# A one-core decoder step: one expert's overflow moved into the last expert step, expert positions swapped by a table, slot table built only when needed

## Chip, cores, metric

One NeuronCore of a Trainium2 chip runs the whole step as one program. The metric is the device time of one execution in microseconds (us), as a median over runs. All numbers of the trace come from one profiled execution.

## The reference, cut to what matters

One hybrid decoder layer over 576 tokens (512 prompt, 64 sample) with 1024 channels, all in float32. A token mixer comes first. Then comes the part that the change touches, a mixture of 16 experts in 4 groups. A token's group is the largest of 4 logits. Inside the group its 2 best experts are taken, so there are 1152 (token, expert) pairs. After it come a gate with a per-token embedding and a last normalisation.

```
gl = (xf @ w_rg + b_rg);  g = argmax(gl);  el_g = expert logits of group g
top_v, top_i = top_k(el_g, 2);  w = softmax(top_v) * g_w;  ids = g * 4 + top_i
for e in range(16):
    h = silu(xf @ w_gate[e]) * (xf @ w_up[e])        # 1024 -> 512
    y = y + combine[:, e:e+1] * (h @ w_down[e])      # 512 -> 1024
```

With the reference's own inputs the pairs of the experts 0 to 15 number, counted by running its router:

```
116 138 113 125  40  34  57  41  54  89  48  77  72  50  50  48
```

One expert has more than 128, expert 1 with 138.

## The kernel before, in words

Tokens lie in five tiles of up to 128 rows (`TILES`). TensorE takes float32 data apart: a weight unit of 1 MB (`UNIT`, 128x2048) is loaded into a ring of six (`raw`, `load_unit`, L446), ScalarE rounds it to `hi` (`split_high`, L867 in the profile), VectorE computes `lo = raw - hi` (`split_low`, L1227), and each product is three matmuls: hi by hi, lo by hi, hi by lo (`split_product`, L1684 to L1686). `hi` and `lo` are rings of three units, so a split waits until TensorE has used the unit three before.

**Router.** VectorE finds the two experts of each token (`first_max`), and two small matmuls (L1998, L1999) give each pair its rank in its expert and each expert's count. Matmuls with one-hot rows (L2005, `pick`, L1499) then list the first 128 tokens of every expert in `lists`, with `NOBODY` where there are fewer. Each pair's slot number goes to `pos`, and GpSimd writes all pairs into a table `slots` in memory by ten indirect DMAs (L795). The table is there for pairs beyond the 128th.

**Experts.** `STEPS` is 17: one step per expert, and a 17th that repeats one expert (`again`, from `jobs_i`) for its ranks 128 to 255, whose list SyncE reads from `slots` (L520, `extra_in`). Where nothing overflows it runs all the same, with expert 0 or an empty list. A step `e0` on TensorE (`step`, L2059) is: gate and up product of expert e0 (four units, 48 matmuls of 512 columns, stationary tokens), transposes of the gathered rows of expert e0+1 (L1695), down product of expert e0-1 (two units, 24 matmuls), transposes of the hidden rows (`transpose_hidden`, L2036). The steps 0 and 1 and the last are written out; the others are a loop on every engine. After the last step the down product of the last expert follows by itself. Should there be more than one overflow job, a slow general path behind `If(jobs_n > 1)` does them.

**GpSimd** gathers rows of expert e0+2 from `normed` (L766, L768) when TensorE has transposed those of e0+1, and scatters results of e0-1 to `pairs` (L775, L777). Its queue is in order, so the ten writes of L795 stand between gather 1 and gather 2. **SyncE** issues all weight loads in order; it loads the first two steps, then waits for `jobs_done` and for all ten slot writes (`slots_out`), then loads on.

**VectorE** in a step splits four units, multiplies `hid` (L1515), subtracts for the gathered rows (L1519), splits two units, subtracts for the hidden rows (L1524), and copies half of a result (L1532). Ahead of step 0 it works out the jobs (L1556 to L1572).

**Tail.** After the last scatter SyncE loads `pairs` into the ring (`pairs_full`, L558), and `head`, `combine`, the gate product and the last normalisation follow, with weights `w_ple_gate` in the units from `N_GATE` on.

`router_parts` (L1918) already uses a form that the change uses too: 32 stationary columns, 128 moving columns, float32 operands without a split, and outputs in four strips of 32 partitions (`LANE`, `LANES`).

```
for c in range(DC):
    lane = slice(c % LANES * LANE, (c % LANES + 1) * LANE)
    ins = mm(bank[5][lane, at:at + r], wr[:, c, :], wide[:, c * P:c * P + r], ...)
```

## Time and profile before

| what | value |
|---|---|
| median of 3 runs | 640.5 us (638.12 to 642.43) |
| the profiled execution | 645.75 us |
| its span, first to last instruction | 644.0 us |
| around the span | 1.75 us |
| mean granted TensorE clock | 0.964 of full |
| TensorE matmul busy | 591.2 us, 92% |
| VectorE, ScalarE, GpSimd busy | 512.1, 362.9, 205.1 us |
| moved by DMA | 153.99 MB |

Where a row has the form "start us, us, engine line op", the first number is the time from the span's start and the second how long the row lasts; in square brackets stands how long the engine was idle before it and what released it. Matmul records overlap, since they are pipelined, so work is measured from start to start. A float32 matmul without a split shows as two records.

### The profile page before, as it was taken

What the parts mean: (1) busy time and instruction counts of PE and PEld (TensorE: products, weight loads), DVE (VectorE), ACT (ScalarE), POOL (GpSimd) and SP (SyncE); (2) the same over time, 40 slices, a digit from 0 to 9 for tenths busy, and PEclk for the clock granted to TensorE, in tenths of its full rate; (3) what the DMA queues carried; (4) which work ended last, traced back from release to release, by engine and by line L of the source; (5) the groups of instructions that cost most, each with busy time, mean ns of one, the idle gap of its engine ahead of it and who ended that gap; (6) DMA issues with size and microseconds to landing.
All of it is one profiled execution on the core that took longest, in us unless ns stands there. A gap on an engine that the chain in (4) does not pass through costs nothing.

```text
span 644.0 us, 9878 instructions
## 1 busy us (share of the span) xinstructions
PE 591.2 (92%) x3434; PEld 509.2 (79%) x3434; DVE 512.1 (80%) x556; ACT 362.9 (56%) x374; POOL 205.1 (32%) x215
## 2 busy tenths in 40 slices
PE   3799999998999888799999999999999999469994
PEld 3799999976787667578888888888888888359993
DVE  4768998996724777689999999999999999497545
ACT  6712322425435627477777787787777778434343
POOL 8153646882200028322212222222221212122004
PEclk9799999998999889899999999999999999859998
DMA  8987221027143245799999999999999999480003
GB/s 255 282 244 254 67 67 66 1 75 248 48 162 131 83 145 180 274 348 387 384 389 388 393 367 364 387 362 376 395 369 380 379 360 369 145 294 3 1 1 147
DMA packets 79075, 153.99 MB, mean 239 GB/s; under 512 B 8413, under 2 KB 26429, under 8 KB 78589
## 3 DMA queue, kind: packets, MB, share of 16 engines
q1 hardware_dynamic: 71637, 138.98, 61.1%
q0 software_dynamic: 5520, 9.56, 4.0%
q10 hardware_dynamic: 1888, 5.05, 2.2%
q8 instruction: 19, 0.31, 0.2%
q14 instruction: 11, 0.09, 0.0%
HBM read 147.91 MB, written 14.41 MB: 252 GB/s over the span
## 4 chain that ended last, share of the span: by engine, by line
PE 80%; DVE 5%; issue 4%; POOL 4%; DMA 4%; SPq 2%; ACT 1%; POOLq 0%; ACTq 0%; DVEq 0%
PE pair L1684 21%; PE pair L1686 20%; PE pair L1685 20%; PE pair L1731 12%; PE pair L1695 3%; POOL slots L795 2%; DVE pair L1275 1%; DMA two<-normed,few 1%; SPq L470 1%; PE pair L2036 1%; DVE lo L1227 1%; DMA two<-in_state_conv 1%; DMA two<-normed,vecs 1%; ACT hi L867 1%; PE pair L1857 0%
## 5 line engine op out<-in xcount | busy, mean ns | idle before, releaser
L1684 PE MATMUL pair<-hi,act_hi 128*128 128x512 f32 (+3 forms) x748 | 276.7, 370 | 4.4 <-DVE act_lo L1524 2.6
L1227 DVE TENSOR_TENSOR lo<-raw,hi 128x2048 fp32r<-128x2048 f32 x111 | 251.5, 2291 | 34.8 <-ACT hi L867 34.7
L1686 PE MATMUL pair<-hi,act_lo 128*128 128x512 f32 (+3 forms) x748 | 269.1, 360 | 0.0
L1685 PE MATMUL pair<-lo,act_hi 128*128 128x512 f32 (+3 forms) x748 | 269.0, 360 | 0.0
L867 ACT ACTIVATE hi<-raw 128x2048 fp32r<-128x2048 f32 x119 | 224.9, 1916 | 51.1 <-PE pair L1686 25.1
L1684 PEld LDWEIGHTS pair<-hi,act_hi 128*128 128x128 f32 (+1 forms) x748 | 140.2, 187 | 31.1 <-DVE lo L1227 4.9
L1686 PEld LDWEIGHTS pair<-hi,act_lo 128*128 128x128 f32 (+1 forms) x748 | 139.7, 187 | 22.4 <-issue 0.4
L1685 PEld LDWEIGHTS pair<-lo,act_hi 128*128 128x128 f32 (+1 forms) x748 | 140.3, 188 | 19.3 <-issue 0.2
L777 POOL DMA_INDIRECT pairs<-two,few x17 | 43.2, 2540 | 111.7 <-DVE two L1532 111.7
L1275 DVE SCALAR_TENSOR_TENSOR pair<-conv,vecs,pair 128x512 f32<-128x512 f32 x112 | 74.9, 749 | 0.0
L867 ACT ACTIVATE act_hi<-pair 128x1024 fp32r<-128x1024 f32 (+3 forms) x50 | 38.1, 781 | 65.1 <-PE pair L1695 38.7
L1731 PE MATMUL pair<-act_hi,hi 128*128 128x288 f32 x192 | 42.2, 302 | 0.0
L1731 PE MATMUL pair<-act_hi,lo 128*128 128x288 f32 x192 | 41.9, 301 | 0.0
L1731 PE MATMUL pair<-act_lo,hi 128*128 128x288 f32 x192 | 41.8, 300 | 0.0
L766 POOL COPY few<-vecs 128x1 uint32 (+1 forms) x16 | 10.0, 626 | 92.8 <-PE pair L1695 92.8
L615 POOL TENSOR_TENSOR lo<-raw,hi 128x2048 fp32r<-128x2048 f32 x6 | 27.7, 4619 | 24.1 <-ACT hi L867 24.1
L1695 PE MATMUL pair<-ident,two 128*128 128x128 f32 (+1 forms) x208 | 27.9, 279 | 7.1 <-DMA two<-normed,few 4.4
L1695 PEld LDWEIGHTS pair<-ident,two 128*128 128x128 f32 (+1 forms) x208 | 24.4, 146 | 10.3 <-DMA two<-normed,few 4.8
L1731 PEld LDWEIGHTS pair<-act_hi,hi 128*128 128x128 f32 x192 | 31.9, 195 | 0.0
L1731 PEld LDWEIGHTS pair<-act_lo,hi 128*128 128x128 f32 x192 | 31.7, 193 | 0.0
L1731 PEld LDWEIGHTS pair<-act_hi,lo 128*128 128x128 f32 x192 | 31.7, 193 | 0.0
L1519 DVE TENSOR_TENSOR act_lo<-pair,act_hi 128x1024 fp32r<-128x1024 f32 x17 | 20.7, 1217 | 8.8 <-ACT act_hi L867 8.8
(221 smaller groups left out, 503.3 us busy)
## 6 DMA issues: line engine op xcount, KB each, us to landing
raw<-in_w_exp_gate SPq DMA_DIRECT2D x34, 1024.0 KB, 8.3
raw<-in_w_exp_up SPq DMA_DIRECT2D x34, 1024.0 KB, 8.9
raw<-in_w_exp_down SPq DMA_DIRECT2D x34, 1024.0 KB, 9.9
h<-in_x_prompt SPq DMA_DIRECT2D x8, 512.0 KB, 7.3
raw<-in_w_in SPq DMA_DIRECT2D x8, 512.0 KB, 7.4
raw<-in_w_in SPq DMA_DIRECT2D x4, 1024.0 KB, 10.1
raw<-in_w_out SPq DMA_DIRECT2D x4, 1024.0 KB, 7.9
raw<-in_w_ple_gate SPq DMA_DIRECT2D x4, 1024.0 KB, 10.3
```

Of the source, the lines that this page charges most:

```text
L615: nc.gpsimd.tensor_tensor(lo[:, n % SPLIT, :], raw[:, n % RAW, :], hi[:, n % SPLIT, :].bitcast(F32), ALU.subtract).then_inc(lo_pool, 1)
L777: nc.gpsimd.indirect_dma_start(pairs, bass.IndirectOffsetOnAxis(sidx[:, :], 0), res, None, bounds_check=last_pair, oob_is_err=False).then_ ...
L795: nc.gpsimd.indirect_dma_start(slots, bass.IndirectOffsetOnAxis(pos[0:rows(t), t, k:k + 1], 0), pays[0:rows(t), t, k, :], None).then_inc(s ...
L867: return nc.scalar.activation(out_, in_, ACT.Copy)
L1227: nc.vector.tensor_tensor(lo[:, n % SPLIT, :], raw[:, n % RAW, :], hi[:, n % SPLIT, :].bitcast(F32), ALU.subtract).then_inc(lo_dve, 1)
L1275: nc.vector.scalar_tensor_tensor(out=to, in0=src, scalar=w, in1=conv_acc[k % 2], op0=ALU.mult, op1=ALU.add).then_inc(acc, 1)
L1519: nc.vector.tensor_tensor(xlo, pair[1][:, :].rearrange("p (c n) -> p c n", c=DC), xhi.bitcast(F32), ALU.subtract).then_inc(g_lo, 1)
L1684: mm(out_, x_hi, w_hi, start=start, stop=False)
L1685: mm(out_, x_hi, w_lo, start=False, stop=False)
L1686: return mm(out_, x_lo, w_hi, start=False, stop=stop)
L1695: ins = tr(to[:, c * P:c * P + r], src[0:r, c * P:(c + 1) * P], ident[0:r, 0:r])
L1731: ins = mm(outs[s], w[:, c, cols], x[:, c, s * HALF:(s + 1) * HALF], start=(c == 0 and w is w_hi and x is ahi), stop=(c == DC - 1 and last))
```

## The change

- `STEPS` is 16: one step per expert, no repeated one.
- **Order of the experts.** The router's columns are loaded with their halves swapped, so that position s holds expert (s + 8) mod 16 (`expert_at`); `rev` gets a second row, so that ties are still resolved as before. Four positions are fixed (`FIXED`). Of the other twelve (`OPEN`) the first one with 129 to 160 pairs changes places with the last position; a small table (`entry`: list columns and expert number) is swapped by VectorE, and SyncE reads the expert number of each position from `order` before its loads (`expert_in`).
- **Overflow in the last step.** Ranks 128 to 159 of that expert (`SPILL` = 32 tokens) are done in the last step from the raw units while they are in the ring, in float32 without a split, in four strips of 32 output partitions: 32 tokens stationary, 128 columns of weights moving for gate and for up (32 matmuls each), 256 columns for down (16 matmuls). SyncE loads the two down units of the last expert only when the gate part is done (`spill_pe`, `SP_GATE`), and the `w_ple_gate` units only when the up part is (`SP_UP`). Results go to `pairs` in quarters of a row by one more scatter.
- **Slot table.** The ten writes L795, the slot numbers (L1502 to L1504) and the job codes are now inside `If(jobs_n > 1)`. `jobs_n` counts overflow beyond what the last step does, plus one.
- The router's four small loads become eight; some semaphores are merged.

```diff
-STEPS = EXPERTS + 1
+STEPS = EXPERTS
+FIXED = 4
+OPEN = EXPERTS - FIXED
+SPILL = 32
...
+            sp.wait_ge(lists_in, 2)
+            this = expert_in(slice(0, 1))
...
+            with sp.Fori(0, OPEN - 1) as d:
+                last = expert_in(bass.ds(d, 1))
+                this = expert_in(bass.ds(d + 1, 1))
+                for k in range(6):
+                    load_unit(step_unit(FIXED + 1, k), d, this if k < 4 else last)
+            this = expert_in(slice(OPEN - 1, OPEN))
+            sp.wait_ge(spill_pe, SP_GATE)
+            for n in range(N_GATE - 2, N_GATE):
+                load_unit(n, 0, this)
...
-            sp.wait_ge(slots_out, 16 * 2 * TILES)
-            sp.dma_start(lists[:, EXPERTS, :], slots[bass.ds(at, P), :]).then_inc(extra_in, 16)
...
+            sp.wait_ge(spill_pe, SP_UP)
             for n in range(N_GATE, N_UNITS):
                 load_unit(n)
```

GpSimd:

```diff
             gather(1)
-            g.wait_ge(slots_clear, 16)
-            g.wait_ge(const, N_LATE)
-            g.wait_ge(slot_at, 1)
-            for t in range(TILES):
-                for k in range(2):
-                    nc.gpsimd.indirect_dma_start(
-                        slots, bass.IndirectOffsetOnAxis(pos[0:rows(t), t, k:k + 1], 0),
-                        pays[0:rows(t), t, k, :], None).then_inc(slots_out, 16)
             gather(2)
...
             step(STEPS - 3)
+            g.wait_ge(spill_dve, SP_LISTED)
+            nc.gpsimd.indirect_dma_start(spill_rows, None, normed, bass.IndirectOffsetOnAxis(spill_at[0:SPILL, 0:1], 0),
+                                         bounds_check=last_token, oob_is_err=False).then_inc(spill_in, 16)
...
             scatter(STEPS - 2)
+            g.wait_ge(spill_dve, SP_RES)
+            nc.gpsimd.indirect_dma_start(pairs.rearrange("n (j d) -> (n j) d", j=LANES),
+                                         bass.IndirectOffsetOnAxis(spill_at[:, 1:2], 0), spill_res, None,
+                                         bounds_check=last_quarter, oob_is_err=False).then_inc(spill_out, 16)
```

VectorE and TensorE, new functions:

```diff
             step(0)
+            spill_picks()
             step(1)
-            with v.Fori(0, STEPS - 3) as d:
-                step(2, d)
-            step(STEPS - 1)
+            step(2)
+            spill_lists()
+            with v.Fori(0, STEPS - 4) as d:
+                step(3, d)
+            last_step(STEPS - 1)
...
+            def spill_gate_up(n, at):
+
+                for c in range(DC):
+                    w = raw[:, (n + c // (DC // 2)) % RAW, c % (DC // 2) * DE:(c % (DC // 2) + 1) * DE]
+                    for i in range(LANES):
+                        ins = mm(bank[5][i * LANE:(i + 1) * LANE, at:at + P], spill_x[:, c * SPILL:(c + 1) * SPILL],
+                                 w[:, i * P:(i + 1) * P], start=(c == 0), stop=(c == DC - 1))
+                ins.then_inc(spill_pe, 1)
...
+            def last_step(e0):
+
+                n = step_unit(e0, 0)
+                spill_transpose()
+                gate_half(n, e0, 0)
+                pe.wait_ge(spill_act, SP_ROWS_SB)
+                spill_gate_up(n, 2 * P)
+                gate_half(n, e0, 1)
+                spill_gate_up(n + 2, 3 * P)
+                down(step_unit(e0, 4), e0 - 1)
+                spill_inner()
+                transpose_hidden(e0)
+                spill_down(N_GATE - 2)
+                down(N_GATE - 2, e0)
```

`spill_transpose` turns the 32 gathered rows (8 transposes, 32 columns out), `spill_inner` the 128x128 hidden block (1 transpose). `spill_list`, 5 matmuls of 2 columns, stands on TensorE between step 1 and step 2 and makes the list of the 32 tokens.

GpSimd's queue from gather 1 to gather 3, before (L766 and L768 are a gather, L795 the slot writes):

```order
L766 COPY few<-vecs 128x1 [waits g_ps,gathered]
L768 DMA two<-normed,few 128x1024 [waits gidx_set,x_in0]
L795 DMA slots<-conv,vecs 10240x2 [waits slot_at,const,slots_clear]
L795 DMA slots<-conv,vecs 10240x2 x9
L766 COPY few<-vecs 128x1 [waits g_ps,gathered]
L768 DMA two<-normed,few 128x1024 [waits gidx_set,x_in0]
```

The same place after (L817 and L819 are a gather, L826 and L828 a scatter):

```order
L838 DMA two<-normed,vecs 128x1024 [waits gidx_set,lists_in]
L817 COPY few<-vecs 128x1 [waits g_ps,gathered]
L819 DMA two<-normed,few 128x1024 [waits gidx_set,x_in0]
L817 COPY few<-vecs 128x1 [waits g_ps,gathered]
L819 DMA two<-normed,few 128x1024 [waits gidx_set,x_in0]
```

Gather 2 now stands right behind gather 1.

VectorE between step 0 and step 1, before (L1524 is the end of step 0, the four L1227 are the first splits of step 1):

```order
L1519 TENSOR_TENSOR act_lo<-pair,act_hi 128x1024 [waits g_hi]
L1227 TENSOR_TENSOR lo<-raw,hi 128x2048 [waits pe_unit,hi_done]
L1524 TENSOR_TENSOR act_lo<-pair,act_hi 128x512 [waits t_hi]
L1227 TENSOR_TENSOR lo<-raw,hi 128x2048 [waits pe_unit,hi_done] x4
L1515 TENSOR_TENSOR work<-pair,work 128x512 [waits t_ps,pe_unit,silu_done]
```

The same place after (L1625 ends step 0, L1307 are the splits):

```order
L1625 TENSOR_TENSOR act_lo<-pair,act_hi 128x512 [waits t_hi]
L1671 TENSOR_SCALAR ones<-pair 1x16 x3
L1673 TENSOR_TENSOR conv<-conv 128x120
L1675 TENSOR_REDUCE conv<-ones 1x1 [waits dve]
L1676 TENSOR_REDUCE conv<-conv 128x10
L1677 TENSOR_SCALAR conv<-conv 1x1 [waits dve]
L1678 SCALAR_TENSOR_TENSOR conv<-vecs,conv 128x10
L1680 TENSOR_TENSOR conv<-conv 128x10
L1682 COPY conv<-conv 128x5 [waits dve]
L1683 TENSOR_TENSOR conv<-conv 128x5
L1684 SCALAR_TENSOR_TENSOR conv<-conv 128x5
L1687 TENSOR_SCALAR wide<-place,conv 128x128 [waits dve]
```

Seventeen instructions (the last row's five, of which one is shown) now stand between the end of step 0 and the first split of step 1.

ScalarE's last step, before (L867 with `hi` is a split, L1070 the silu of the last expert):

```order
L867 ACTIVATE hi<-raw 128x2048 [waits pe_unit,raw_in3]
L1070 ACTIVATE work<-pair 128x512 [waits hid_done,pe_unit]
L867 ACTIVATE hi<-raw 128x2048 [waits pe_unit,raw_in4]
L867 ACTIVATE hi<-raw 128x2048 [waits pe_unit,raw_in5]
L867 ACTIVATE hi<-raw 128x2048 [waits pe_unit,raw_in0]
L867 ACTIVATE act_hi<-pair 128x512 [waits t_ps]
```

The same place after (L1170 is the silu of the 32 tokens; `wide` holds their data):

```order
L925 ACTIVATE hi<-raw 128x2048 [waits pe_unit,raw_in3]
L1128 ACTIVATE work<-pair 128x512 [waits hid_done,pe_unit]
L925 ACTIVATE hi<-raw 128x2048 [waits pe_unit,raw_in4]
L1170 ACTIVATE wide<-pair 128x128 [waits spill_pe]
L925 ACTIVATE hi<-raw 128x2048 [waits pe_unit,raw_in5]
L925 ACTIVATE hi<-raw 128x2048 [waits pe_unit,raw_in0]
L925 ACTIVATE wide<-pair 128x128 [waits spill_pe]
L925 ACTIVATE act_hi<-pair 128x512 [waits t_ps]
```

The two splits for the last down product now stand behind the silu of the 32 tokens, which waits for the up strips, and the hidden block of the 32 tokens is copied ahead of the last expert's own.

## Rows read from the trace of the kernel before

**Rows 1.** The page's sections 1 and 4: engine's busy time, and the ending chain's shares.

```profile
PE 591.2 (92%) x3434; PEld 509.2 (79%) x3434; DVE 512.1 (80%) x556; ACT 362.9 (56%) x374; POOL 205.1 (32%) x215
PE 80%; DVE 5%; issue 4%; POOL 4%; DMA 4%; SPq 2%; ACT 1%; POOLq 0%; ACTq 0%; DVEq 0%
```

**Rows 2.** Chain in order of time, hidden transposes ending steps 2 and 15.

```profile
297.88 0.44 PE pair L2036 x4
...
531.01 0.44 PE pair L2036 x4
```

**Rows 3.** Chain in order of time, 239 to 273 us, around the slot table.

```profile
239.14 1.36 POOL slots L795
...
258.41 2.07 POOL few L766
...
261.27 9.41 DMA two<-normed,few
270.73 1.97 PE pair L1695 x8
```

**Rows 4.** TensorE's waits, 205 to 300 us: total, times, longest.

```profile
PE pair L1695 <- DMA two<-normed,few: 4.4, 1, 4.4
```

**Rows 5.** TensorE's windows of 1 us: stretch, length, busy (records), granted clock, DMA share, GB/s.

```profile
269.00:270.00 1.00, 0.00 (x0) 0.79 1.04 404
270.00:271.00 1.00, 0.27 (x2) 0.50 1.06 412
...
276.00:277.00 1.00, 1.00 (x5) 0.79 1.00 397
...
550.00:551.00 1.00, 0.00 (x0) 1.00 0.99 312
```

**Rows 6.** TensorE in order of time, first matmul of step 1; weight load of its third unit.

```profile
254.87 0.47 PE L1684 MATMUL pair<-hi,act_hi 128*128 128x512 f32 x1 [1.78 <-issue]
...
260.55 0.19 PEld L1684 LDWEIGHTS pair<-hi,act_hi 128*128 128x128 f32 x1 [0.18 <-issue]
```

**Rows 7.** VectorE in order of time, 225 to 263 us: small operations and splits.

```profile
225.53 0.24 DVE L1497 TENSOR_REDUCE vecs<-conv 128x5 f32<-128x80 f32 x1
227.32 1.07 DVE L1499 TENSOR_SCALAR work<-place,vecs 128x128 f32<-128x128 f32 x5
230.03 0.74 DVE L1556 TENSOR_SCALAR ones<-pair 1x16 f32<-1x16 f32 x4
233.09 2.29 DVE L1227 TENSOR_TENSOR lo<-raw,hi 128x2048 fp32r<-128x2048 f32 x1
237.78 1.22 DVE L1519 TENSOR_TENSOR act_lo<-pair,act_hi 128x1024 fp32r<-128x1024 f32 x1 [2.40 <-ACT act_hi L867]
258.15 4.48 DVE L1227 TENSOR_TENSOR lo<-raw,hi 128x2048 fp32r<-128x2048 f32 x2
```

**Rows 8.** Chain: router strips and their next matmul; TensorE's small rank matmuls.

```profile
197.78 0.57 PE pair L1918 x16
198.35 0.43 PE pair L1684
223.53 0.39 PE L1999 MATMUL pair<-conv,ones 128*128 128x80 f32 x2
223.75 0.33 PE L2000 MATMUL pair<-conv,ones 128*128 128x16 f32 x2
```

**Rows 9.** TensorE's waits, 530 to 575 us: total, times, longest.

```profile
PE pair L1684 <- DVE act_lo L1524: 2.6, 1, 2.6
```

**Rows 10.** DMA issues by line: count, KB each, median us to landing.

```profile
raw<-in_w_exp_down SPq DMA_DIRECT2D x34, 1024.0 KB, 9.9
raw<-in_w_ple_proj SPq DMA_DIRECT2D x1, 1024.0 KB, 4.7
```

**Rows 11.** GpSimd in order of time, the last gather and scatters, 509 to 563 us.

```profile
519.75 0.09 POOL L806 MEMSET few<- 1x1 f32 x1
551.60 0.97 POOL L777 DMA_INDIRECT pairs<-two,few  x1 [7.39 <-DVE two L1532]
556.05 0.18 POOL L775 COPY few<-vecs 128x1 uint32<-128x1 uint32 x1 [3.48 <-DMA pairs<-two,few]
```

More of the change, by code:

```diff
@@ L93, with expert_at @@
 MIX, FFN, GATE, FINAL = range(4)
+N_LISTED = N_LATE + 5
+SP_LIST, SP_ROWS, SP_GATE, SP_UP, SP_INNER, SP_DOWN = range(1, 7)
+SP_ROWS_SB, SP_SILU, SP_INNER_SB = range(1, 4)
+GENERAL = 6 + 1 + OVERFLOW_MAX + 6
+SP_PICKED, SP_LISTED, SP_MUL, SP_RES = range(TILES, TILES + 4)
+def expert_at(s):
+    return (s + EXPERTS // 2) % EXPERTS
 def rows(t):
@@ L319, in hybrid_layer @@
         jobs_done = sem("jobs_done")
+        spill_pe = sem("spill_pe")
+        spill_act = sem("spill_act")
+        spill_dve = sem("spill_dve")
+        spill_in = sem("spill_in")
+        spill_out = sem("spill_out")
         v_idx = sem("v_idx")
-        v_w = [sem(f"v_w{i}") for i in range(3)]
+        v_w = sem("v_w")
         v_in = sem("v_in")
@@ L388, in unit_source @@
                 k, e = 4 + (n - N_STEP - 6 * (STEPS - 1)), STEPS
-            e = e + d
-            if again is not None:
-                e = again if k < 4 else again + 1
+            expert = which if which is not None else expert_at(e if k < 4 else e - 1)
             if k < 4:
@@ L445, in _, with load_unit @@
         def _(sp):
-            def load_unit(n, d=0, again=None):
+            def load_unit(n, d=0, which=None):
                 if n >= RAW:
@@ L450, in load_unit @@
                     wait_all(sp, (hi_done, done), low_done(n - RAW, d))
-                src = unit_source(n, d, again)
+                src = unit_source(n, which)
                 if n < CB:
@@ L816, in _ @@
             g.wait_ge(jobs_done, 1)
-            jobs_n = g.value_load(jobs_i[0:1, 2 * OVERFLOW_MAX:], min_val=0, max_val=OVERFLOW_MAX)
+            jobs_n = g.value_load(jobs_i[0:1, NJ - 1:], min_val=0, max_val=OVERFLOW_MAX + 1)
             with g.If(jobs_n > 1):
+                g.wait_ge(slots_clear, 16)
+                g.wait_ge(const, N_LATE)
+                g.wait_ge(slot_at, GENERAL)
+                for t in range(TILES):
+                    for k in range(2):
+                        nc.gpsimd.indirect_dma_start(
+                            slots, bass.IndirectOffsetOnAxis(pos[0:rows(t), t, k:k + 1], 0),
+                            pays[0:rows(t), t, k, :], None).then_inc(slots_out, 16)
                 g.wait_ge(gathered, 16 * STEPS)
@@ L1486, in _ @@
             v.wait_ge(const, N_LATE)
-            link(nc.vector.memset(zeros, 0.0))
             for k, m in enumerate((M1, M2)):
@@ L2054, in down, with spill_list, spill_transpose @@
                     ins.then_inc(pe_unit, 1)
+            def spill_list():
+                pe.wait_ge(spill_dve, SP_PICKED)
+                for t in range(TILES):
+                    ins = mm(bank[5][:, 0:2], spill_pick[0:rows(t), t, :], payS[0:rows(t), t, :],
+                             start=(t == 0), stop=(t == TILES - 1))
+                ins.then_inc(spill_pe, 1)
+            def spill_transpose():
+                pe.wait_ge(spill_in, 16)
+                pe.wait_ge(spill_dve, SP_LISTED)
+                for c in range(DC):
+                    ins = tr(bank[5][:, c * SPILL:(c + 1) * SPILL], spill_rows[:, c * P:(c + 1) * P],
+                             ident[0:SPILL, 0:SPILL])
+                ins.then_inc(spill_pe, 1)
@@ new lines, in spill_down @@
+            def spill_down(n):
+                pe.wait_ge(hi_done, n + 2)
+                pe.wait_ge(spill_act, SP_INNER_SB)
+                for c in range(CB):
+                    w = raw[:, (n + c // 2) % RAW, c % 2 * D:(c % 2 + 1) * D]
+                    for i in range(LANES):
+                        ins = mm(bank[2][i * LANE:(i + 1) * LANE, 0:2 * P], spill_h[:, c * SPILL:(c + 1) * SPILL],
+                                 w[:, i * 2 * P:(i + 1) * 2 * P], start=(c == 0), stop=(c == CB - 1))
+                ins.then_inc(spill_pe, 1)
```

304 lines of the change are left out of this document (209 added, 95 removed).

## The prediction

> **What bounds the kernel now.** I read the page first: TensorE's matmuls are busy for 92% of the span, and TensorE makes 80% of the chain that ended last [rows 1]. Then the chain in order of time. From step 2 on it holds nothing but TensorE, and the hidden transposes come back at an even distance: from 297.88 to 531.01 us there are 13 steps, 233.13 us, so 17.93 us a step [rows 2]. A step has 72 matmuls of 512 columns and 12 transposes, the latter at 0.11 (0.44 for four), so a matmul is 16.6 / 72 = 0.23 us, and there is no room for a wait. A step removed is worth its full length, and work added to TensorE in a step costs its full length. The chain leaves TensorE ahead of step 2, where GpSimd and a DMA hold it, and after the last product. The waits of TensorE give the size of these holes, its windows of 1 us the clock in them. A change of about 1% is what a measurement of this kernel can tell from none.
>
> **1. One step fewer.** 16 steps instead of 17: -17.93 us [rows 2]. Its weight loads, gather and scatter go with it.
>
> **2. The slot table leaves GpSimd's queue.** Before, the ten writes run from 239.14 to 258.41, then the gather of step 2 goes, and TensorE gets its rows at 270.73 [rows 3] after 4.4 us of waiting [rows 4], idle since 266.3. The granted clock falls from 2.4 to 1.2 GHz at 269.8 and is back at 276.2 [rows 5]; TensorE works for 5.5 of these us and loses half of them, 2.8. The place costs 7.2 us in all. After, gather 2 stands right behind gather 1. It waits for the transposes of step 1's rows, which end before step 1's first matmul at 254.87 [rows 6], so it is issued at about 254, and even with the 9.41 us that the DMA has in the chain [rows 3] it lands by 264, before TensorE asks. SyncE's wait for the table is gone too, so step 2's units come earlier. The 7.2 us would all be gained if nothing came in their place.
>
> **What comes in their place** is VectorE. Between the end of step 0 and the first split of step 1 now stand 17 small instructions. TensorE needs that split at once: before, the first of the two splits at 258.15 ends 2.25 us later, at 260.4 [rows 7]. TensorE, from 254.87 on, has worked through two units by then (24 x 0.23 = 5.5), and its weight load of the third unit follows at 260.55, already 0.18 late [rows 6]. There is no slack. The 17 by rows: three of 1x16 at 0.19; two of 128x120 at about 0.3, above the 0.24 of one of 80 columns; a reduction of 1x64 and one of 1x1, together 0.35; five of 128x5 or 128x10 at 0.2, little above the 0.19; five picks 1.07 [rows 7]. That makes 0.57 + 0.6 + 0.35 + 1.0 + 1.07 = 3.6 us. TensorE stands still for 3.6 us, from 260.4 to 264.0. The 4.4 us before brought the low clock after some 3.5 us of idleness; the 2.6 us in the last step did not, the clock is at full at 550 to 551 [rows 5, 9]. 3.6 lies between. I take it that the clock falls, for about 4 us of work: 2.0 us lost.
>
> The Trainium skill speaks against this part (TensorE: Matmul & The Clock Gate, "HAM oscillation"): an idle gap between bursts makes the array start again at half clock. By that rule alone the loss is certain; by the row at 550 a gap can also pass without it.
>
> The later splits do not add to it: VectorE does the four of step 1 in a row until 271.0, at 2.25 each, and TensorE takes them at 264.0, 266.7, 270.6 and 273.3. Five matmuls of 2 columns (the list) stand on TensorE after step 1. A lone matmul of 80 columns keeps the next one 0.22 us away [rows 8], so 1.1 us at most; at the strips' 0.07 it is 0.35. I take 0.9. The loss up to step 2's gate product is then 3.6 + 2.0 + 0.9 = 6.5 us where it was 7.2: **-0.7**. Ends: clock holds and the list is short, 3.95, so -3.3; clock low as long as before (2.8) and the list 1.1, 7.5, so +0.3.
>
> Ahead of step 0 the chain of the swap has 18 VectorE operations at about 0.21, 3.9 us from 229.9 on, so the split behind it starts at 233.8 instead of 233.09 and ends at 236.1. The next instruction there is the subtraction for gathered rows at 237.78, which waited 2.40 for ScalarE [rows 7]: nothing. In the loop only two value loads of SyncE per step are new; units are asked for 13 us ahead or more and land in 9.9 [rows 10]: nothing, at most 1 us in all. The two operations of `spill_lists`, 0.4 us once, fall into VectorE's wait for ScalarE ahead of the next split. The small loads early on delay SyncE while TensorE has its units: nothing.
>
> **3. The last step grows.** The strips have the form of the router's: 8 matmuls, 32 stationary and 128 moving columns, take 0.57 us, and the matmul behind them takes 0.43 instead of 0.23, so 0.2 for coming back [rows 8]. Gate: 32 matmuls, 4 x 0.57 + 0.2 = 2.5. Up: 2.5. Down: 16 of 256 columns, as much streaming, 2.5. Eight transposes of 32 rows: full ones are at 0.11 [rows 2], 0.9 at most, I take 0.7. One 128x128 transpose: 0.15. Sum 8.35 us. Against it stands the wait that the last step has before, 2.6 us, until the last expert's hidden rows are taken apart [rows 9]. The down strips now run in it. They need the 32 tokens' hidden block, copied by ScalarE some 0.8 us behind its transpose; the last expert's own transposes (0.44) cover half of that hop. So 8.35 - 2.6 + 0.4 = **+6.1**.
>
> Is the last down product late for its weights? Its two loads now wait for the gate strips, 0.7 + 24 x 0.23 + 2.5 = 8.7 us into the step. ScalarE wants the first after the up strips, 8 us later. A 1 MB load landed in 4.7 us where the queue was quiet and in 9.9 in the median of the down units [rows 10]. Little else loads then, so both are there in time, and the splits on ScalarE and VectorE run beside the 5.5 us of the down product before. If they take 9.9: +1.5. The units of `w_ple_gate` come as 4 MB together behind the up strips, some 16 us before they are wanted.
>
> The ends for the strips: if the four did not overlap, each matmul would cost the 0.22 of the lone one [rows 8], 80 x (0.22 - 0.07) = +12.0 over my sum. I take the router's price, the same shape in the same kernel. The Trainium skill (TensorEngine Tiling (Array Packing), "Key Properties") says that changing the tiling mode drains TensorE; the row shows a small size for it, the 0.2 us at the return.
>
> The 32 rows' gather goes out where GpSimd has its memset at 519.75 [rows 11], and the last step begins at 531.5 [rows 2]. With up to 9.4 us to land it comes 2 us early. A miss costs what it misses by.
>
> **4. The end.** The copies of the last result wait for the scatter before it. Before, that one was issued at 551.60 and had let go of the buffer by 556.05 [rows 11], in 4.4 us. After, it goes out some 5 us before the last product ends, with 4 MB of gate weights in flight: +0.3, up to 2. The strips' scatter lands beside it. The tail behind is the same code.
>
> **Sum.** -17.93 - 0.7 + 6.1 + 0.3 = **-12.2 us**. The profiled execution took 645.75, so it would take 633.5. It lies 5.25 above the median of the runs shown; from that median, 640.5 - 12.2 = 628.3 us.
>
> **The rivals.**
> - *The new gap is cheap* (clock holds, list short): -2.6 more, 625.7. For it: 3.6 us is not far above 2.6. Against: the weight load at 260.55 has no slack. Chance 0.13.
> - *The last step is held up*: the 32 rows come late, the down units take 9.9 each, and the scatter before the last holds the result, 1.5 each: +4.5, 632.8. For it: margins of 2 us. Against: less is in flight there than in the loop. Chance 0.12.
> - *The strips do not overlap*: +12.0, 640.3, no gain. Against: 0.57 us for eight is a third of 8 x 0.22. Chance 0.05.
> - *The change doesn't do what it says, the general path runs.* Place: `jobs_n` > 1 behind the last step. It decides from a count above 160, or above 128 in a fixed position, or a second expert above 128. Price: ten slot writes 19.3 [rows 3], a gather 9.4, 24 matmuls of 512 columns at no less than 0.23, 5.5, a scatter 4.4: 38.6 over the forecast, 667, slower. The trace of before shows no such path, but would not show one count between 129 and 255. The reference's inputs tell it: one expert above 128, with 138, and it is expert 1, position 9 of the new order. Chance 0.02.
>
> The forecast has the other 0.68, by itself 624.5 to 632.
>
> **Range and chances.** The first two rivals belong in the range, the third only if half true: 622.5 to 634.5. Faster by over 1% means below 634.1: the forecast, the first rival and nearly all of the second, with room for what I have not seen, 0.90. Within 1%: 0.07. Slower: 0.03.
>
> **What would show it.** Right: 16 steps at 17.93; the slot writes gone, and no wait of TensorE for step 2's rows; a new wait of 3.6 us two units into step 1, with half clock behind it; groups of 32 strip matmuls at 2.3 us; no wait ahead of the last down product, and 31 us from the last step's start to its end. Wrong: a step of other length, strips at more than 3 us a group, TensorE waiting in the last step for rows or weights, or loads of expert weights behind it.

## The result, and the profile of the changed kernel

The changed kernel takes 631.41 us (median of 4 runs, 630.93 to 631.75) where the kernel before took 640.06 beside it (4 runs, 638.12 to 642.43): ratio 0.9863, with 0.9828 to 0.9897 as its 95% interval, so 8.65 us faster, where 12.2 were forecast (628.3). The two profiled executions lie further apart than the medians: 631.6 us (span 629.8) against 645.75 (span 644.0), 14.2 us. That difference between 8.65 and 14.2 turned out to be the main thing to explain.

The first two rows answer to [rows 1]: TensorE has the same share of the span, 92%, and a slightly greater one of the ending chain; GpSimd is gone from it.

```profile
PE 579.8 (92%) x3529; PEld 500.2 (79%) x3529; DVE 494.6 (79%) x563; ACT 350.1 (56%) x367; POOL 184.2 (29%) x208
...
PE 82%; DVE 6%; DMA 4%; issue 2%; SPq 2%; ACT 2%; POOL 0%; POOLq 0%; DVEq 0%; ACTq 0%
```

The chain in order of time (start us, us, what), for [rows 2]. L2193 is the hidden block's transposes, L1846 the transposes of gathered rows, L2217 the list matmuls:

```profile
268.51 0.87 PE pair L1846 x8
274.86 0.44 PE pair L2193 x4
275.30 1.10 PE pair L2217 x10
...
312.00 0.44 PE pair L2193 x4
317.90 0.43 PE pair L1835
...
509.25 0.44 PE pair L2193 x4
```

From 312.00 to 509.25 lie 11 steps, 17.93 us each: the loop's step is unchanged. The list costs 1.1 us. The row at 317.90 is the 25th matmul of a gate and up product: it takes 0.43 in every step, with no strips near it, which bears on the last step below.

GpSimd in order of time, for [rows 3]: gather 2 is issued at 253.11 (forecast 254) and nothing waits for it.

```profile
237.80 1.04 POOL L819 DMA_INDIRECT two<-normed,few  x1 [0.78 <-POOL few L817]
...
253.11 1.02 POOL L819 DMA_INDIRECT two<-normed,few  x1 [0.76 <-POOL few L817]
```

VectorE between step 0 and the third unit of step 1, for [rows 7]; the seventeen small instructions run from 257.73 to 260.36, in 2.63 us (forecast 3.6):

```profile
243.01 4.50 DVE L1307 TENSOR_TENSOR lo<-raw,hi 128x2048 fp32r<-128x2048 f32 x2 [4.00 <-ACT hi L925]
...
257.73 0.31 DVE L1671 TENSOR_SCALAR ones<-pair 1x16 f32<-1x16 f32 x3
257.97 0.26 DVE L1673 TENSOR_TENSOR conv<-conv 128x120 f32<-128x120 f32 x1
...
259.37 1.07 DVE L1687 TENSOR_SCALAR wide<-place,conv 128x128 f32<-128x128 f32 x5
260.36 4.49 DVE L1307 TENSOR_TENSOR lo<-raw,hi 128x2048 fp32r<-128x2048 f32 x2
```

TensorE's waits from 205 to 300 us (total, times, longest), for [rows 4]. The wait for gathered rows of the kind `few` is gone, and the new one is for VectorE's split, 1.0 at its longest. The "issue" wait, 1.8, is the one behind step 0.

```profile
PE pair L1835 <- issue: 1.8, 1, 1.8
...
PE pair L1835 <- DVE lo L1307: 1.2, 2, 1.0
```

Its windows of 1 us (columns as in [rows 5]): the granted clock falls behind the 1.8 us wait, before the stall.

```profile
254.00:255.00 1.00, 0.56 (x3) 1.00 1.05 410
255.00:256.00 1.00, 1.00 (x4) 0.53 0.85 314
...
258.00:259.00 1.00, 1.00 (x5) 0.77 0.25 76
...
261.00:262.00 1.00, 0.76 (x4) 1.00 0.73 281
```

So TensorE does eight of its first eleven matmuls of step 1 at 1.2 GHz, comes to the third unit later, and the stall is hardly 1 us: the low clock hides most of it. In the second profile of the same kernel (`a_again`, below) it is the other way round, a stall of 2.4 us and the clock low behind it.

The last step, in the chain (L2226 turns the 32 gathered rows, L2235 is a strip group, 32 matmuls that show as 64 records):

```profile
509.69 0.61 PE pair L2226 x8
510.30 0.43 PE pair L1835
...
515.98 1.88 PE pair L2235 x64
517.87 0.43 PE pair L1835
...
523.53 1.89 PE pair L2235 x64
525.41 0.43 PE pair L1835
```

From one group to the next are 7.55 us, 24 matmuls at 0.227 (5.46) and 2.09 for the group with the slower first matmul behind it. The matmul at 517.87 is the 25th of the step, which takes 0.43 in an ordinary step too (317.90 above), so its 0.2 is no price of the gate strips.

And the end of it, where the chain leaves TensorE. L1633 is VectorE's half of a result, `pairs<-two,few` a scatter, `raw<-pairs` the tail's load, L1786 the first `combine`:

```profile
534.71 6.39 DMA pairs<-two,few
...
541.20 0.70 DVE two L1633
...
542.68 5.33 DMA pairs<-two,few
...
548.18 4.30 DMA raw<-pairs
...
552.58 0.76 DVE h L1786
```

TensorE's last product ends at about 539.9, but the copy of its result starts at 541.20: it waits for the scatter before it. The last scatter then takes 5.3 us.

### The profile page after: what moved, and what is told of

The parts are those of the page before. It is cut to its first block, busy times and chain, and to the rows that moved or that the text cites. A ratio compares the mean times of both kernels' runs of the same rounds, so it can differ in the third digit from the quotient of the medians.

```text
span 629.8 us, 10009 instructions
## 1 busy us (share of the span) xinstructions
PE 579.8 (92%) x3529; PEld 500.2 (79%) x3529; DVE 494.6 (79%) x563; ACT 350.1 (56%) x367; POOL 184.2 (29%) x208
## 4 chain that ended last, share of the span: by engine, by line
PE 82%; DVE 6%; DMA 4%; issue 2%; SPq 2%; ACT 2%; POOL 0%; POOLq 0%; DVEq 0%; ACTq 0%
PE pair L1835 21%; PE pair L1837 20%; PE pair L1836 20%; PE pair L1882 12%; PE pair L1846 3%; DMA pairs<-two,few 2%; DVE lo L1307 2%; DVE pair L1357 2%; SPq L495 1%; ACT hi L925 1%; DMA two<-in_state_conv 1%; PE pair L2193 1%; DMA two<-normed,vecs 1%; DMA raw<-pairs 1%; PE pair L2235 1%
## 5 line engine op out<-in xcount | busy, mean ns | idle before, releaser
L1835 PE MATMUL pair<-hi,act_hi 128*128 128x512 f32 (+3 forms) x724 | 266.7, 368 | 3.5 <-issue 2.3
L1307 DVE TENSOR_TENSOR lo<-raw,hi 128x2048 fp32r<-128x2048 f32 x105 | 237.8, 2290 | 40.3 <-ACT hi L925 39.9
L1837 PE MATMUL pair<-hi,act_lo 128*128 128x512 f32 (+3 forms) x724 | 259.5, 358 | 0.0
L1836 PE MATMUL pair<-lo,act_hi 128*128 128x512 f32 (+3 forms) x724 | 259.1, 358 | 0.0
L925 ACT ACTIVATE hi<-raw 128x2048 fp32r<-128x2048 f32 x113 | 213.8, 1914 | 53.8 <-PE pair L1837 27.5
L1835 PEld LDWEIGHTS pair<-hi,act_hi 128*128 128x128 f32 (+1 forms) x724 | 135.5, 187 | 29.0 <-issue 5.1
L1837 PEld LDWEIGHTS pair<-hi,act_lo 128*128 128x128 f32 (+1 forms) x724 | 135.1, 187 | 21.5 <-issue 0.2
L1836 PEld LDWEIGHTS pair<-lo,act_hi 128*128 128x128 f32 (+1 forms) x724 | 135.7, 187 | 18.5 <-issue 0.2
L828 POOL DMA_INDIRECT pairs<-two,few x16 | 40.3, 2517 | 112.3 <-DVE two L1633 105.4
L817 POOL COPY few<-vecs 128x1 uint32 (+1 forms) x15 | 7.9, 529 | 107.8 <-PE pair L1846 107.8
L1846 PE MATMUL pair<-ident,two 128*128 128x128 f32 (+1 forms) x200 | 26.2, 275 | 2.3 <-DMA two<-normed,vecs 2.3
L1236 ACT ACTIVATE wide<-pair,rs 128x256 f32<-128x256 f32 (+1 forms) x20 | 9.4, 472 | 32.2 <-PE pair L1837 32.2
L1846 PEld LDWEIGHTS pair<-ident,two 128*128 128x128 f32 (+1 forms) x200 | 23.2, 145 | 5.1 <-issue 2.9
```

What stands on the lines that cost most here:

```text
L817: nc.gpsimd.tensor_copy(gidx[:, :], lists[:, bass.ds(e0 + d, 1), 0]).then_inc(gidx_set, 1)
L828: nc.gpsimd.indirect_dma_start(pairs, bass.IndirectOffsetOnAxis(sidx[:, :], 0), res, None, bounds_check=last_pair, oob_is_err=False).then_ ...
L925: return nc.scalar.activation(out_, in_, ACT.Copy)
L1236: nc.scalar.activation(wide[0:r, (q % 4) * UC:(q % 4 + 1) * UC], bank[4 + q % 4][0:r, 0:UC], ACT.Sigmoid, scale=rs[0:r, GATE, t:t + 1]).th ...
L1307: nc.vector.tensor_tensor(lo[:, n % SPLIT, :], raw[:, n % RAW, :], hi[:, n % SPLIT, :].bitcast(F32), ALU.subtract).then_inc(lo_dve, 1)
L1835: mm(out_, x_hi, w_hi, start=start, stop=False)
```

## The experiments

The expectations speak of theories by letters. Theory A is that the 7.2 us of [rows 3 to 5] (4.4 of waiting, 2.8 of low clock) belonged to the one execution that was profiled; Theory E is that the last result waits for a buffer that the scatter before it still reads.

To compare places, each profile is cut at four marks, each the start of a row in order of time (TensorE's, and VectorE's for the last): the transposes of gather 0 (step 0 can start), those of gather 2 (step 2's rows are there), those of the last gather, and the first `combine` behind the last scatter. All in us:

| profile | start to gather 0 | to gather 2 | to last gather | to first combine | tail | span |
|---|---|---|---|---|---|---|
| before | 235.08 | 35.65 | 253.77 | 41.95 | 77.55 | 644.0 |
| b_again | 233.12 | 32.63 | 251.11 | 43.79 | 77.55 | 638.2 |
| after | 234.75 | 33.60 | 234.39 | 49.84 | 77.22 | 629.8 |
| a_again | 234.41 | 35.23 | 234.35 | 49.49 | 77.12 | 630.6 |
| a_nostrip | 234.88 | 33.66 | 234.41 | 43.82 | 76.93 | 623.7 |
| a_picks | 233.13 | 32.42 | 234.41 | 49.78 | 76.46 | 626.2 |
| a_picks_list | 234.37 | 31.02 | 233.32 | 49.69 | 76.40 | 624.8 |
| a_own | 232.41 | 35.23 | 234.44 | 48.64 | 77.48 | 628.2 |
| a_best | 233.22 | 30.74 | 233.27 | 48.54 | 77.33 | 623.1 |
| b_table_late | 233.12 | 32.39 | 251.22 | 43.80 | 76.27 | 636.8 |
| b_newloads | 233.01 | 31.03 | 252.04 | 43.83 | 76.59 | 636.5 |
| b_full | 232.62 | 33.23 | 252.60 | 43.57 | 76.98 | 639.0 |

### b_again: the kernel before, profiled once more

No edit.

> The kernel before once more, for a second profile. The median fell by 8.65 us where the two profiled executions are 14.15 apart, and the profiled execution of before lay 5.7 us above its median. Theory A: the 4.4 us wait of TensorE for the gather of step 2, and the low clock behind it, belong to slow slot writes (0.91 to 3.09 us each, 19.3 us in all) and are no fixed part of the kernel. Then an execution near 640 us shows writes that end 4 to 6 us earlier, a wait of under 1 us there and the clock at full behind it. Rival B: the wait is always there and the 5.7 us lie elsewhere (early DMAs or the tail). Then the wait shows 4 to 5 us again even at 640.

Measured: 640.45 us (638.19 to 642.15, 10 runs), ratio 0.9998 [0.9973, 1.0023]; its profiled execution took 639.92, 5.8 less than the first one. GpSimd's queue in it, against [rows 3]:

```profile
237.51 1.36 POOL L795 DMA_INDIRECT slots<-conv,vecs  x1 [0.30 <-issue]
...
241.84 2.71 POOL L795 DMA_INDIRECT slots<-conv,vecs  x1 [0.30 <-issue]
...
253.01 0.89 POOL L795 DMA_INDIRECT slots<-conv,vecs  x1 [0.30 <-issue]
...
256.50 2.91 POOL L768 DMA_INDIRECT two<-normed,few  x1 [0.80 <-POOL few L766]
```

The ten writes run from 237.51 to 253.90, 16.4 us, where the first profile has 19.3 and begins 1.6 later. TensorE's wait for the rows:

```profile
PE pair L1695 <- DMA two<-normed,few: 0.2, 1, 0.2
```

0.2 us instead of 4.4, and no low clock behind it. So the 7.2 us are no fixed part of the kernel, which is Theory A's main point: the table's writes end just about when TensorE asks. How slow the writes are is not all that decides. The profile of `b_full` (below; same table, same place) has writes that end at 253.38, before those of `b_again`, and yet TensorE waits 2.0 us for the same rows, with the low clock behind that wait. There the clock held behind step 0's wait and TensorE came early, at 263.8; in `b_again` it fell, TensorE came at 265.6, and the low clock swallowed the wait. In `b_newloads` the writes end at 252.57, the clock holds, and there is no wait at all: 31.03 us up to gather 2. In other places the profile of `b_again` loses where the first one did not, as TensorE's windows show:

```profile
253.00:254.00 1.00, 1.00 (x4) 0.74 0.02 1
254.00:255.00 1.00, 1.00 (x4) 0.50 0.02 1
...
542.00:543.00 1.00, 0.00 (x0) 1.00 1.09 367
543.00:544.00 1.00, 0.61 (x2) 0.81 0.84 270
544.00:545.00 1.00, 1.00 (x3) 0.50 0.28 100
```

The clock fell behind step 0's wait, and behind the 2.6 us wait of the last step, which it passed at full in [rows 5].

### b_table_late: the table out of the way, and nothing else

In the kernel before, three slot writes each go behind the scatters of steps 1 and 2, four behind that of step 3, and the 17th step's list is loaded by GpSimd.

```diff
             gather(2)
             step(1)
+            slot_writes(0, 3)
+            step(2)
+            slot_writes(3, 6)
+            step(3)
+            slot_writes(6, 10)
...
-            sp.wait_ge(slots_out, 16 * 2 * TILES)
-            sp.dma_start(lists[:, EXPERTS, :], slots[bass.ds(at, P), :]).then_inc(extra_in, 16)
```

> Part 2 of the change alone, without its price: the kernel before with the ten slot writes spread behind the scatters of steps 1 to 3, and the list of the 17th step loaded from GpSimd's queue after them; SyncE no longer waits for them. 17 steps as before. Theory A (the wait is mostly absent in a median run): 1 to 3 us under before, 637 to 639. Rival B (the 7.2 us are there in every run): 7 us under before, 633. Either way gather 2 is issued at about 254 and TensorE does not wait for it.

Measured: 639.65 us (637.61 to 642.39, 12 runs), ratio 0.9983 [0.9962, 1.0003]. What the table cost in its place is 1.1 us of 640 by the ratio, and the interval holds zero. The writes cost nothing in their new place that shows: from gather 2 to the last gather are 251.22 us, against 251.11 in `b_again`. The 7.2 us are not there to be had.

### a_nostrip and a_nostrip_early: what the strips cost

The changed kernel without the overflow's strips, transposes, copies and the two waits of SyncE, so that ten pairs' results are not worked out; the scatter of the strips' results stays, with other data (`a_nostrip`), or goes ahead of the last two scatters (`a_nostrip_early`).

```diff
             def last_step(e0):
...
-                spill_transpose()
                 gate_half(n, e0, 0)
-                spill_gate_up(n, 2 * P)
                 gate_half(n, e0, 1)
-                spill_gate_up(n + 2, 3 * P)
                 down(step_unit(e0, 4), e0 - 1)
-                spill_inner()
                 transpose_hidden(e0)
-                spill_down(N_GATE - 2)
```

> The changed kernel with the 32 tokens' rows, strips, silu, product and copies left out of the last step, and with SyncE's two waits for the strips; their last scatter stays where it is and carries other data. It leaves out the work of the overflow tokens. The trace of the changed kernel shows the last step 7.9 us longer than before's from its start to the first combine. Theory: 4.4 us of it is TensorE, the rest is the result waiting for the scatter ahead of it and slower scatters and loads beside the gate weights. Then this kernel saves 5 to 6 us on the changed one, about 626, and keeps a slower last scatter. Rival (all 7.9 comes from the strips and their waits): 623.5.

> As the one before, with the 32 tokens' scatter moved ahead of the last step, so that nothing of the overflow stands behind the last scatters. Theory: the extra scatter costs 1 to 2 us where it stands, so 624 to 625. Rival (the scatter is covered, the gate weights alone slow the end): the same as with the scatter in its place, within 0.5 us.

Measured: 624.79 us (624.56 to 625.48), ratio 0.9739 [0.9712, 0.9767], and 624.9 (623.39 to 628.33), 0.9755 [0.9718, 0.9791]. The strips cost 6.3 to 6.6 us, a little more than the 5 to 6 expected, against the 631.1 to 631.4 of the two measurements of the changed kernel (7.0 to 7.9 by the ratios, since the kernel before was 641.28 beside this run). The end of `a_nostrip` in the chain:

```profile
535.23 0.70 DVE two L1621
...
536.72 5.20 DMA pairs<-two,few
...
546.77 0.76 DVE h L1770
```

By the marks the strips cost 49.84 - 43.82 = 6.0, in two pieces: TensorE ends its last product 37.16 us behind the last gather's transposes instead of 32.25, +4.9; the copy and the issue behind it take 2.78 us instead of 1.49, +1.3, because the wait for the buffer appears only when the strips' product and scatter are there. The first piece, from the same rows, is 0.8 for the transposes of the 32 rows, 4.0 for the gate and up strips together, and 0.1 for the block's transpose; from the hidden transposes to the end both kernels take the same (531.02 to 539.44 here, 526.29 to 534.80 in `a_nostrip`), so the down strips are wholly covered. The place of the strips' scatter is worth nothing that shows, as the rival had it.

### a_again: the changed kernel, profiled once more

> The changed kernel once more, beside the variants of it. 631.4 as before, within 1 us; the profile again with TensorE reaching the first gathered rows at 234 to 235 us, a stall of 1 us for the third unit of step 1, and the last result held by the scatter ahead of it.

Measured: 631.07 us (629.11 to 632.37, 5 runs), ratio 0.9848 [0.9825, 0.9871]. Its waits from 205 to 300 us:

```profile
PE pair L1835 <- DVE lo L1307: 2.4, 1, 2.4
...
PE pair L1835 <- issue: 1.8, 1, 1.8
```

Here the clock held behind the 1.8 us wait, so TensorE came early to the third unit and waited 2.4, not the 1 expected, and the clock fell there, from 262.7 to 265.5. The part up to gather 2 costs 35.23 against 33.60. Which of the two waits brings the low clock differs from one execution to the next.

### a_picks and a_picks_list: the new work put beside waits

`a_picks` moves the seventeen instructions on VectorE ahead of step 0, where they fall into waits for ScalarE; `a_picks_list` also moves the list matmuls on TensorE from behind step 1 to behind step 0, into the 1.8 us wait.

```diff
 VectorE:
+            spill_picks()
             step(0)
-            spill_picks()
...
 TensorE:
             step(0)
+            spill_list()
             step(1)
-            spill_list()
```

> The 17 VectorE instructions of the overflow's one-hot rows moved from behind step 0 to ahead of it, where VectorE waits 4.0 us for ScalarE in the changed kernel's trace. Theory C (they stand on the chain between the steps 0 and 1 and are covered ahead of step 0): the stall of 1.0 us in step 1 goes, 0.8 to 1.5 us less, 630.2. Rival D (TensorE comes late to that unit anyway, because the clock is low; only the clock matters): the same time within 0.4 us.

> As the one before, and the five list matmuls moved from behind step 1 to behind step 0, into TensorE's wait of about 2 us for step 1's rows. Theory C: their 1.1 us are covered there, and with the wait partly filled the clock may hold, 1.6 more: 628 to 629.5. Rival D: the wait behind step 0 grows by what is put into it, nothing gained on the one before.

Measured: 628.27 us (627.75 to 629.26), ratio 0.9816 [0.9795, 0.9838], and 627.05 (624.83 to 629.44), 0.98 [0.9773, 0.9827]. TensorE's waits in `a_picks_list`:

```profile
PE pair L1835 <- issue: 0.7, 1, 0.7
...
PE pair L1835 <- DVE lo L1307: 0.2, 1, 0.2
```

The picks' place costs 2.8 us (631.07 to 628.27), more than the 0.8 to 1.5 expected, and the stall is gone but for the 0.2 that the kernel before has too. The runs of the two kernels hardly touch, 627.75 to 629.26 against 629.11 to 632.37. By the marks up to gather 2 it is 1.2 against `after`, which like `a_picks` has the low clock behind step 0, and 2.8 against `a_again`, which has the longer stall. The list's place shows in the profile: the part up to the last gather falls by 1.1, to 13 steps of 17.93 and 0.2. In the times it is 1.2 (627.05, below the 628 to 629.5 expected) with overlapping intervals, so the times alone don't show it.

### a_own: the last result in a buffer of its own

The last result is copied to the gathered rows' buffer, free by then, so its copy waits for no scatter.

```diff
-            result(N_GATE - 1, STEPS - 1)
+            wait_used(v, N_GATE - 1)
+            nc.vector.tensor_copy(xg[:, C:], bank[7]).then_inc(res_dve, 1)
...
-            scatter(STEPS - 1)
+            nc.gpsimd.indirect_dma_start(pairs, bass.IndirectOffsetOnAxis(lists[:, STEPS - 1, 1:2], 0), xg, None, ...
```

> The last result gets a buffer of its own (the gather's, which is free by then), and its scatter reads its index straight from the list; so neither waits for the scatter ahead of it. Theory E (in the changed kernel the copies wait from the end of the product, about 539.3, to 541.2 for that scatter): 1.9 us less, 629.5; the last scatter goes out right behind the product. Rival F (the scatters and the gate weights share the DMA engines, so an earlier one only takes longer): less than 0.7 us gained.

Measured: 629.83 us (627.19 to 630.12), ratio 0.9826 [0.9802, 0.9851], overlapping with `a_again`. The profile is clearer. The chain behind the product, which ends at 539.19:

```profile
539.21 0.70 DVE two L1714
...
540.68 5.37 DMA pairs<-two,vecs
```

The copy follows at once, the part to the first `combine` is 48.64 instead of 49.84 or 49.49. Theory E is right in kind and worth about 1 us there, half of the 1.9 expected; the tail, which varies from 76.3 to 77.6 among the profiles, gives it back in part in this one. The scatter itself stays at 5.4.

### b_full: how long the last scatter takes

The kernel before, whose 17th step scatters ten valid rows, with 118 rows of expert 1 added to that scatter's list (it writes over their results).

```diff
+                    nc.gpsimd.tensor_copy(sidx[:, :], lists[:, 1:2, 1]).then_inc(sidx_set, 1)
+                    wait_all(g, (sidx_set, e0 + 1))
+                    nc.gpsimd.tensor_copy(sidx[0:10, :], lists[0:10, e0:e0 + 1, 1]).then_inc(sidx_set, 1)
```

> The kernel before, with its last scatter (the 17th step's) given 128 valid rows instead of 10: ten of its own, and 118 of expert 1's, which it writes over. In every version with 16 steps the last scatter took 5.1 to 5.4 us from issue to landing, in the kernel before 3.7. Theory: that is the number of rows written, because the last step is now the fullest expert's. Then it takes 5.2 to 5.4 here, the first combine comes 1.5 us later behind the scatter's issue, and the time is about 1.5 above the kernel before. Rival: it is what is in flight beside it (the scatter before, closer now). Then it stays at 3.7 and the time does not move.

Measured: 642.46 us (640.72 to 643.49, 8 runs), ratio 1.0043 [1.0028, 1.0059], +2.5. The last scatter and the load behind it in the chain, here and then in `b_again`:

```profile
552.41 5.07 DMA pairs<-two,few
557.65 4.27 DMA raw<-pairs
```

```profile
552.23 3.68 DMA pairs<-two,few
556.08 4.47 DMA raw<-pairs
```

5.07 us with 128 valid rows, 3.68 with ten: at this place the rows make the difference, and the rival falls. The time does not grow evenly with them, though: the scatter before it, of 48 rows, held its buffer from 543.97 to 549.24 in `b_again`, 5.3 us, and 4.5 in `before`. By the marks the end takes 43.57, against 41.95 in `before`, where the clock held in the last step as it did here: +1.6. The median rose by some 1 us more than the scatter did; that is not explained.

### b_newloads: the eight small router loads

```diff
-            sp.dma_start(wr[:, :, 0:GROUPS], a["w_router_group"][0]...
+                for i in range(2):
+                    here = slice(to + i * n // 2, to + (i + 1) * n // 2)
+                    sp.dma_start(wr[:, :, here], a[w][0]...
```

> The kernel before with the router's four small loads made eight, as the changed kernel has them (same columns, in halves, order of the experts unchanged). If these loads are what makes step 0 start about 1.6 us later in the changed kernel's profile (transposes of gather 0 at 234.8 against 233.1), that marker stands at 234.7 here and the time is about 1.5 above the kernel before. If they are nothing, as forecast, the marker stands anywhere between 232.4 and 235.1, where executions with either set of loads have had it, and the ratio holds 1 in its interval.

Measured: 640.22 us (638.23 to 642.15, 10 runs), ratio 1.0001 [0.9982, 1.0019]; the transposes of gather 0 at 233.01. The loads are nothing. The 1.6 us by which step 0 starts later in `after` than in `b_again` come and go: 232.41 in `a_own`, 234.75 in `after`, 235.08 in `before`.

### a_best: the three moves together

`a_picks_list` and `a_own` in one kernel.

> The three moves that each gained are put together: VectorE's seventeen small instructions ahead of step 0, TensorE's five list matmuls behind step 0, and the last result copied to a buffer of its own so that its scatter does not wait for the one before. If the effects add, since one acts in steps 0 and 1 and the other behind the last product: 627.05 us with the first two, less the 1.2 of the third, about 625.8 us; from the gather-2 transposes back to the gather-0 ones about 31.0 us, and from the last gather's transposes to the first combine 48.5 to 48.7. Rival: the earlier last scatter only lengthens the wait of the tail's load for something else (the strips' scatter, the gate weights), and the pair stays at 627.0; the segment at the end is then 49.5 or more.

Measured: 626.13 us (624.82 to 627.97, 5 runs), ratio 0.9778 [0.9755, 0.9802] to the kernel before, below that of the changed kernel, 0.9848 [0.9825, 0.9871]. In the profile both effects are there: 30.74 us up to gather 2 (31.0 expected), 48.54 from the last gather to the first combine (48.5 to 48.7). In the times the third move is not told from none: 0.9 less than `a_picks_list`, with overlapping intervals. It beats both kernels, the changed one by about 5 us.

## Why the prediction was right and wrong

**The step, -17.93: right.** 11 steps from 312.00 to 509.25 at 17.93 us.

**The slot table and what comes in its place, -0.7: this term failed, above all in the gain.** The prediction counted "the place costs 7.2 us in all" as removed [rows 3 to 5]. That was read from one execution that lay 5.25 us above the median, and the sum was then taken off the median as if every execution had those 7.2. The wait there is 4.4, 0.2, 2.0 and 0 us in the four profiles of a kernel with the table in its place, and moving the table away gains 1.1 us, with zero in the interval (`b_table_late`). The new work costs 3.9 (below). The columns of the table above give the size, with `after` against each of the two profiles of before:

| part | forecast | against before | against b_again |
|---|---|---|---|
| up to gather 0 | 0 | -0.33 | +1.63 |
| to gather 2, and the loop without its step | -0.7 | -3.50 | +2.18 |
| one step | -17.93 | -17.93 | -17.93 |
| last gather to first combine | +6.4 | +7.89 | +6.05 |
| tail | 0 | -0.33 | -0.33 |
| span | -12.2 | -14.2 | -8.4 |

Against the profile it was worked out from, the sum errs by 2.0 the one way; against an execution near the median by 3.8 the other. The change's own time was forecast at 633.5 for a like execution and measured at 631.6. What was wrong is the step from 633.5 to 628.3: part of what the change removes was itself the reason why that execution was long, so it could not be taken off the median again. With the +2.2 measured for this part in place of -0.7 (the row above, against `b_again`) the same sum from the median gives 631.2 us; 631.4 was measured. That it comes so near is luck: +2.2 is one pair of profiles, `a_again` against `b_again` gives +3.8, and the experiments' times give 3.9 - 1.1 = +2.8. An estimate by these: -17.93 + 2.8, +7.7 for the last step and the end (49.84 and 49.49 against 41.95), and -1.1, because the kernel before and its variants lose 1.8 us to the low clock behind the last step's 2.6 us wait in three of five profiles, a wait that the change removes: -8.5, where the two measurements have 8.65 and 9.4.

**The new work between steps 0 and 2, forecast 6.5: too high.** VectorE's seventeen took 2.63 instead of 3.6, since the rows of small instructions overlap: the three of 1x16, put at 0.57, have let the next one start 0.24 behind the first. The list took 1.1 instead of 0.9. The low clock was taken as a loss of its own behind the stall. In fact step 0's 1.8 us wait, which stands in [rows 6] and which the prediction passed over, brings it in some executions of either kernel (`b_again`, `after`), and then it swallows most of the stall; where it doesn't (`a_again`), the stall is 2.4 and the clock falls there, as forecast. Taking the work out of the way gained 2.8 (`a_picks`) and 1.1 (the list, by the profile): 3.9 in all.

**The last step, +6.1: the mechanism was right, the size 1.2 too high.** TensorE's part is 4.9 (`after` against `a_nostrip`). The gate and up strips cost 4.0 together, not 5.0, the transposes of the 32 rows 0.8 and the block's 0.1. The down strips (L2251 below) take 1.93, not 2.5, and nothing is left over from them, where the sum had 0.3 (2.5 + 0.4 - 2.6). Both down units were there, and the 32 rows too. The wait of 2.6 is replaced by the down strips and 0.5 of issue. TensorE in order of time:

```profile
530.92 0.27 PE L2242 MATMUL pair<-ident,wide 128*128 128x128 f32 x1
531.02 0.60 PE L2193 MATMUL pair<-ident,work 128*128 128x128 f32 x4
531.65 1.93 PE L2251 MATMUL pair<-raw,wide 128*32 128x256 f32 x32
```

The Trainium skill (TensorEngine Tiling (Array Packing), "Key Properties") says that a change of the tiling mode drains TensorE. No run here shows its price: the 0.2 us that the prediction read as the return stands at the 25th matmul of every step too (317.90), where there are no strips, and the two groups together leave 0.2 beside their 1.9 each, which may be it.

**The end, +0.3: too low by about 2.5.** The wait for the scatter before it is 1.3 (`a_own` removes it). Another 1.4 to 1.6 was not foreseen: the last scatter now writes 128 rows of the fullest expert, where the 17th step wrote ten (`b_full`). With the last step's 1.2 the other way this leaves +1.2 to 1.4 against the profile of before, where +1.5 was measured (7.89 against 6.4). `b_again` lost about 1.8 us of its own to the low clock in the last step (nine matmuls at 0.43 instead of 0.23), and so its +6.05 only looks like a hit for +6.4.

**The rivals.** The gap was neither cheap nor at full price, and the forecast's 628.3 missed by 3.1 us. The table's term erred by about 3, the last step and the end by 1.2 and 2.5 with opposite signs, and the low clock that the kernel before has behind its last wait takes about 1 back. So the time lies in the range partly because errors cancel. Of "held up", one of three parts came true, the held result, at 1.3. The strips do overlap, and the general path did not run: 32 loads each of expert weights. 631.4 lies inside the range given, 622.5 to 634.5, and inside the forecast's own; faster by over 1% holds, 1.37% [1.03, 1.72].

## What to carry to other kernels

A wait seen in one profile is a sample: before its price is taken off a median, profile the kernel a second time, and where the profiled execution is long, look for the excess at the very place that the change removes. Small instructions in front of a split that TensorE wants at once cost about their full length here (2.8 us in the times, 2.63 in the rows), and a few lines up nothing that shows. When the last iteration of a loop changes, look at what its store carries and whose buffer it needs, since nothing behind it hides either.

## What was not expected of the hardware

- The granted clock behind a wait of about 2 us is not settled by the length of the wait. In the last step's 2.6 us wait it fell in `b_again`, `b_table_late` and `b_newloads` and held in `before`, `b_full` and the two kernels without strips. Behind step 0's 1.8 us it fell in six of eleven profiles (`b_again`, `b_table_late`, `after`, `a_picks` and the two without strips) and held in five (`before`, `b_newloads`, `b_full`, `a_again`, `a_own`); with 0.7 us of wait there it held in `a_picks_list` and fell in `a_best`. Behind the wait for gather 0, of 2.1 to 3.1 us, it fell in twelve of the thirteen. It fell behind the 4.4 us in `before`, the longest of these waits, behind the stall of 2.4 in `a_again` and `a_own`, and behind the 2.0 in `b_full`. The Trainium skill (TensorE: Matmul & The Clock Gate, "HAM oscillation") tells of long waits for a DMA, behind which the next matmuls start at half clock each time; the 4.4 us agree, and these traces show it behind much shorter waits too, but not each time. One such stretch at 1.2 GHz lasts 3 to 4 us in most of these rows (6.4 in `before`, behind the 4.4 us), so it costs 1.5 to 2 us.
- Indirect writes of up to 128 rows of 8 bytes take GpSimd's queue 0.89 to 2.71 us each in `b_again` and up to 3.1 in `before`, with the same data: ten of them 15.6 us in `b_newloads`, 16.4 in `b_again` and 19.3 in `before`.
- The last scatter of 128x1024 takes 3.68 us with ten valid rows (`b_again`) and 5.07 with 128 (`b_full`), though the engine's own part is 0.97 in both. It is not in proportion: one of 48 rows took 4.5 and 5.3.
